# PEER selection over 64 candidate places in place of 256, and 16 dots moved one stage earlier

## The reference, cut to what matters

```
q = (xb @ w_q).reshape(t, 8, 2, 128)
s = einsum('thpd,hpkd->thpk', q, sub_keys)        # 8 heads x 2 sides x 128 scores per token
top_s, top_i = top_k(s, 16)                       # first selection, per side
cand_s = top_s[:, :, 0, :, None] + top_s[:, :, 1, None, :]   # 16 x 16 = 256 sums per head
best_s, best_pos = top_k(cand_s, 16)              # second selection
idx  = top_i[side 0] * 128 + top_i[side 1] at best_pos
gate = softmax(best_s)
h = gelu(u_table[idx] . xb)
out = sum_k gate * h * v_table[idx]
```

## Time and profile before

| what | us |
|---|---|
| median of 3 runs (lowest, highest) | 3355.05 (3344.94, 3362.86) |
| the profiled execution, its own time | 3345.05 |
| its span, first to last instruction | 3342.9 |
| PE busy | 2903.2 (87%) |
| DVE busy | 2117.9 (63%) |
| ACT busy | 1227.8 (37%) |
| POOL busy | 417.1 (12%) |

### The profile page before, as it was taken

One profiled execution on the slowest core, in us unless ns is written; L12 is line 12 of the kernel. 1 busy time (PEld: TensorE's weight loads), 2 busy tenths in 40 slices (PEclk: granted clock), 3 DMA queues, 4 the chain that ended last, 5 costly groups with the idle time before them and its releaser, 6 DMA issues. The chain is left out here.

```text
span 3342.9 us, 39660 instructions
## 1 busy us (share of the span) xinstructions
PE 2903.2 (87%) x14455; PEld 2351.1 (70%) x14455; DVE 2117.9 (63%) x3648; ACT 1227.8 (37%) x1680; POOL 417.1 (12%) x386
## 2 busy tenths in 40 slices
PE   7998889999939994788869699989998989998897
PEld 2875557777728652666658489989997977666676
DVE  2247348788832257544443426998888759888887
ACT  2248237777722333000032233333333333333232
POOL 0000010000010001000000000000100025555521
PEclk9999979999969856777779899999999989999999
DMA  7350459999913200000013134667776799999996
GB/s 255 95 202 28 132 227 373 369 370 375 353 63 94 71 0 6 1 0 0 0 47 98 57 112 133 203 200 232 236 229 183 216 314 396 390 387 380 380 355 242
DMA packets 370122, 652.22 MB, mean 195 GB/s; under 512 B 120864, under 2 KB 269600, under 8 KB 349088
## 3 DMA queue, kind: packets, MB, share of 16 engines
q1 hardware_dynamic: 225760, 458.09, 39.5%
q0 software_dynamic: 45792, 166.74, 13.5%
q10 hardware_dynamic: 98400, 25.17, 3.4%
HBM read 567.08 MB, written 82.84 MB: 194 GB/s over the span
## 5 line engine op out<-in xcount | busy, mean ns | idle before, releaser
L169 DVE TENSOR_TENSOR w_low<-raw,w_high 128x1024 fp32r<-128x1024 f32 x362 | 442.9, 1223 | 494.4 <-ACT w_high L160 491.8
L160 ACT CAST w_high<-raw 128x1024 fp32r<-128x1024 f32 x362 | 378.6, 1046 | 497.0 <-PE ps L329 481.5
L327 PE MATMUL ps<-x_high,w_high 128*128 128x384 f32 (+1 forms) x1328 | 466.8, 352 | 12.7 <-DVE x_low L2245 11.3
L329 PE MATMUL ps<-x_high,w_low 128*128 128x384 f32 (+1 forms) x1328 | 463.6, 349 | 0.0
L328 PE MATMUL ps<-x_low,w_high 128*128 128x384 f32 (+1 forms) x1328 | 463.4, 349 | 0.0
L266 DVE TENSOR_TENSOR wide_low<-wide_raw,wide_high 128x2048 fp32r<-128x2048 f32 x138 | 314.3, 2290 | 102.7 <-ACT wide_high L259 102.0
L2290 POOL DMA_INDIRECT sp_rows<-in_u_rows,sp_flat x128 | 187.0, 1461 | 1477.5 <-DVE sp_flat L2566 834.2
L327 PE MATMUL ps<-w_high,po_both_high 128*128 128x512 f32 x768 | 312.2, 407 | 50.9 <-DVE po_both_low L2751 50.8
L328 PE MATMUL ps<-w_low,po_both_high 128*128 128x512 f32 x768 | 306.4, 399 | 0.0
L329 PE MATMUL ps<-w_high,po_both_low 128*128 128x512 f32 x768 | 306.4, 399 | 0.0
L259 ACT CAST wide_high<-wide_raw 128x2048 fp32r<-128x2048 f32 x138 | 263.2, 1912 | 76.1 <-DMA wide_raw<-in_w_experts 57.0
(11 more groups left out here) (525 smaller groups left out, 5326.7 us busy)
## 6 DMA issues: line engine op xcount, KB each, us to landing
wide_raw<-in_w_experts SPq DMA_DIRECT2D x138, 1024.0 KB, 8.0
raw<-in_u SPq DMA_DIRECT2D x128, 512.0 KB
raw<-in_v SPq DMA_DIRECT2D x128, 512.0 KB
ada_raw<-in_ada_w SPq DMA_DIRECT2D x24, 1024.0 KB, 5.0
hbuf<-ph_h SPq DMA_DIRECT2D x128, 192.0 KB
gbuf<-ph_staged ACTq DMA_DIRECT2D x6, 4096.0 KB, 33.3
xT<-hbuf SPq DMA_DIRECT2D x128, 192.0 KB
xT<-gbuf SPq DMA_DIRECT2D x128, 192.0 KB
```

The source lines that it names most:

```text
L160: self.m.nc.scalar.copy(self.m.w_high[:, n % AHEAD, :], self.m.raw[:, n % RAW, :]).then_inc(self.m.high_done, 1)
L169: self.m.nc.vector.tensor_tensor(self.m.w_low[:, n % AHEAD, :], self.m.raw[:, n % RAW, :], self.m.w_high[:, n % AHEAD, :].bitcast(F32), AL ...
L327: nc.tensor.matmul(out, w[0], a[0], start=start, stop=False, **more)
L329: return nc.tensor.matmul(out, w[1], a[0], start=False, stop=stop, **more)
```

## The change

In `choose`, half 0 now makes the first selection for all 16 head sides (ten steps), and half 1 the second selection for all 8 heads. The second selection runs over the 64 places of four strips (first rank, number of ranks, width): 16 + 24 + 16 + 8 places, which hold every pair with (a+1)(b+1) at most 16. The place is turned back into the two ranks by two shifts and ten small float instructions. The comparison with 0 to 15 (`eq`) is made for all heads at once, one side after the other. `finish` and `place` stay. 64 dots are made in `peer_hidden` (four more in the choices c = 2 to 5, twelve in the `LAST_ROWS`) and 64 in `peer_output`, in seven rows of twelve, the last in row 108.

```
-CHOOSE_DOTS = {2: (4, 9), 3: (4, 9), 4: (1, 3, 5, 7, 9), 5: (1, 3, 5, 7, 9), 6: (1, 3, 5, 7, 9), 7: (1, 3, 5, 7, 9)}
-EARLY_DOTS = 48
+CHOOSE_DOTS = {2: (2, 5, 8), 3: (2, 5, 8), 4: (1, 3, 5, 7, 8, 9), 5: (1, 3, 5, 7, 8, 9), 6: (1, 3, 5, 7, 9),
+               7: (1, 3, 5, 7, 9)}
+EARLY_DOTS = 64
+PAIRS = 64
+STRIPS = ((0, 1, 16), (1, 3, 8), (4, 4, 4), (8, 8, 1))
...
+                if half == 0:
+                    for side in range(2):
...                      (max, match_replace, max, max_index, max_index for 8 head sides, step 5*side .. 5*side+4)
+                    return
+                nc.vector.tensor_copy(idxf[:], idx[:])
+                for a0, rows, width in STRIPS:
+                    ins = nc.vector.tensor_tensor(cand[...] of [P, HEADS, rows, width] ..., ALU.add)
+                link(ins)
+                every(HEADS, max over cand)            ; step(0)
+                every(HEADS, match_replace)            ; step(1)
+                every(HEADS, max over crest)           ; step(2)
+                every(HEADS, max_index over cand)      ; step(3)
+                every(HEADS, max_index over crest)
+                difference for the gates; two shifts; copies to float, two links
+                step(4)
+                ten small float instructions [P, 8, 16], seven links
+                step(5)
+                for side, out in enumerate((i_, j_)):
+                    link(is_equal into eq [P, 8, 16, 16])   ; step(6 + 2 * side)
+                    link(eq * indices)                      ; step(7 + 2 * side)
+                    link(tensor_reduce)
...
                 for _ in range(LAST_ROWS[c - CHOICES] if c >= CHOICES else 0):
                     row(r)
                     r += 1
+                    sparse.dot(dve, next(dots))
...
 def dot_rows():
-        if r % 6 != 5 and s < SLOTS_EACH:
+        if r * 7 // 12 != (r - 1) * 7 // 12 and s < SLOTS_EACH:
             rows[r].append(s)
```

More of the change, by code:

```diff
@@ L2332, in peer_hidden @@
     QUADS, QUADS_EACH = HALF_TILE // QUAD, ROUND // QUAD
-    K, HH = TOPK, HEADS // 2
+    K = TOPK
     BATCH = 16
@@ L2341, in peer_hidden @@
         rest = sb("rest", [P, HEADS, KEYS])
[L2342 to L2347, removed]
+        val, idx, idxf = (sb(n, [P, 2 * HEADS, K], dt) for n, dt in (("val", F32), ("idx", U32), ("idxf", F32)))
+        cand, crest = sb("cand", [P, HEADS, PAIRS]), sb("crest", [P, HEADS, PAIRS])
+        best, pos, part = sb("best", [P, HEADS, K]), sb("pos", [P, HEADS, K], U32), sb("part", [P, 2, HEADS, K], U32)
+        whole, parts, ranks = (sb(n, [P, a, HEADS, K]) for n, a in (("whole", 1), ("parts", 2), ("ranks", 2)))
+        e4 = crest[:].rearrange("p h c -> p (h c)").rearrange("p (a h k) -> p a h k", a=len(STRIPS), k=K)
+        eq = sb("eq", [P, HEADS, K, K])
         i_, j_, g_ = (sb(n, [P, 2, HEADS, K]) for n in "ijg")
@@ L2512, in choose @@
                 tt = ORDER[n]
-                mine = slice(half * HH, (half + 1) * HH)
-                gates_out = sparse.gate[:].rearrange("p (h k) -> p h k", k=K) if n == 0 else g_[:, (n - 1) % 2]
[L2515 to L2524, removed]
-                step(4)
-                link(nc.vector.tensor_copy(idxf[:], idx[:]))
-                pairs = val[:].rearrange("p (h s) k -> p h s k", s=2)
@@ L2528, in choose @@
[L2528 to L2531, removed]
-                step(5)
-                every(HH, lambda a: nc.vector.match_replace(crest[:, a, :], best[:, a, 0:8], cand[:, a, :], NEG))
@@ L2534, in choose @@
[L2534 to L2547, removed]
-                sides = idxf[:].rearrange("p (h s) k -> p s h k", s=2)
@@ L2549, in choose @@
[L2549 to L2555, removed]
@@ L2556, in choose @@
-                link(ins)
-                for side, out in enumerate((i_, j_)):
-                    ins = nc.vector.tensor_reduce(out[:, (n - 1) % 2, mine, :], eq[:, side], AX.X, ALU.add)
-                link(ins)
-                step(9)
+                if half == 0:
+                    for side in range(2):
+                        some = [side * HEADS + a for a in range(HEADS)]
+                        top = scores[:, tt]
+                        every(HEADS, lambda a: nc.vector.max(val[:, some[a], 0:8], top[:, some[a], :]))
+                        step(5 * side)
+                        every(HEADS, lambda a: nc.vector.match_replace(rest[:, a, :], val[:, some[a], 0:8],
+                                                                       top[:, some[a], :], NEG))
+                        step(5 * side + 1)
+                        every(HEADS, lambda a: nc.vector.max(val[:, some[a], 8:16], rest[:, a, :]))
+                        step(5 * side + 2)
+                        every(HEADS, lambda a: nc.vector.max_index(idx[:, some[a], 0:8], val[:, some[a], 0:8],
+                                                                   top[:, some[a], :]))
+                        step(5 * side + 3)
+                        every(HEADS, lambda a: nc.vector.max_index(idx[:, some[a], 8:16], val[:, some[a], 8:16],
+                                                                   rest[:, a, :]))
+                        step(5 * side + 4)
+                    return
@@ new lines, in choose @@
+                nc.vector.tensor_copy(idxf[:], idx[:])
+                pairs = val[:].rearrange("p (h s) k -> p h s k", s=2)
+                at = 0
+                for a0, rows, width in STRIPS:
+                    ins = nc.vector.tensor_tensor(
+                        cand[:, :, at:at + rows * width].rearrange("p h (a b) -> p h a b", b=width),
+                        pairs[:, :, 0, a0:a0 + rows].unsqueeze(3).to_broadcast([P, HEADS, rows, width]),
+                        pairs[:, :, 1, 0:width].unsqueeze(2).to_broadcast([P, HEADS, rows, width]), ALU.add)
+                    at += rows * width
@@ new lines, in choose @@
+                link(ins)
+                every(HEADS, lambda a: nc.vector.max(best[:, a, 0:8], cand[:, a, :]))
+                step(0)
+                every(HEADS, lambda a: nc.vector.match_replace(crest[:, a, :], best[:, a, 0:8], cand[:, a, :], NEG))
+                step(1)
+                every(HEADS, lambda a: nc.vector.max(best[:, a, 8:16], crest[:, a, :]))
+                step(2)
+                every(HEADS, lambda a: nc.vector.max_index(pos[:, a, 0:8], best[:, a, 0:8], cand[:, a, :]))
@@ new lines, in choose @@
+                step(3)
+                every(HEADS, lambda a: nc.vector.max_index(pos[:, a, 8:16], best[:, a, 8:16], crest[:, a, :]))
+                gates_out = sparse.gate[:].rearrange("p (h k) -> p h k", k=K) if n == 0 else g_[:, (n - 1) % 2]
+                nc.vector.tensor_tensor(gates_out, best[:], best[:, :, 0:1].to_broadcast([P, HEADS, K]), ALU.subtract
+                                        ).then_inc(diffed, 1)
+                for k, bits in enumerate((3, 2)):
+                    ins = nc.vector.tensor_scalar(part[:, k], pos[:], bits, None, ALU.logical_shift_right)
@@ new lines, in choose @@
+                nc.vector.tensor_copy(whole[:, 0], pos[:])
+                link(ins)
+                link(nc.vector.tensor_copy(parts[:], part[:]))
+                step(4)
+                p_, a_, b_ = whole[:, 0], ranks[:, 0], ranks[:, 1]
+                link(nc.vector.tensor_scalar(a_, parts[:, 0], -1.0, 0.0, ALU.add, ALU.max))
+                link(nc.vector.scalar_tensor_tensor(out=a_, in0=parts[:, 1], scalar=-6.0, in1=a_, op0=ALU.add, op1=ALU.max))
+                link(nc.vector.scalar_tensor_tensor(out=a_, in0=p_, scalar=-48.0, in1=a_, op0=ALU.add, op1=ALU.max))
@@ new lines, in choose @@
+                for k, (_, _, width) in enumerate(STRIPS):
+                    ins = nc.vector.scalar_tensor_tensor(out=e4[:, k], in0=a_, scalar=-float(width), in1=p_, op0=ALU.mult,
+                                                         op1=ALU.add)
+                link(ins)
+                link(nc.vector.scalar_tensor_tensor(out=b_, in0=e4[:, 1], scalar=-8.0, in1=e4[:, 0], op0=ALU.add,
+                                                    op1=ALU.max))
+                link(nc.vector.scalar_tensor_tensor(out=b_, in0=e4[:, 2], scalar=-24.0, in1=b_, op0=ALU.add, op1=ALU.max))
@@ new lines, in choose @@
+                link(nc.vector.scalar_tensor_tensor(out=b_, in0=e4[:, 3], scalar=-48.0, in1=b_, op0=ALU.add, op1=ALU.max))
+                step(5)
+                iota16 = m.iota[:, 0:K].unsqueeze(1).unsqueeze(1).to_broadcast([P, HEADS, K, K])
+                sides = idxf[:].rearrange("p (h s) k -> p s h k", s=2)
+                for side, out in enumerate((i_, j_)):
+                    link(nc.vector.tensor_tensor(eq[:], ranks[:, side].unsqueeze(3).to_broadcast([P, HEADS, K, K]), iota16,
+                                                 ALU.is_equal))
+                    step(6 + 2 * side)
+                    link(nc.vector.tensor_tensor(eq[:], eq[:], sides[:, side].unsqueeze(2).to_broadcast([P, HEADS, K, K]),
```

(3 more changed lines are left out.)

## The result

The changed kernel took 3315.2 us in the median of 4 runs (3308.4 to 3320.44), the kernel before 3349.99 (4 runs, 3342.16 to 3362.86): ratio 0.9889, 95% interval 0.9859 to 0.9919. In a second group of runs on one chip, 6 of the changed kernel against 11 of the one before, the ratio was 0.9925 (0.9906 to 0.9944). Both intervals hold the forecast, 3325 for 3355.05, which is 0.9910. The change is thus a gain of about 1%, clear of the noise.

The account below looks back on a forecast made before the run. Bounds: TensorE waiting for VectorE at the hidden stage's gates, DMA in the first 96 output rows. Choices -10, late rows +1, transition +5, output rows -26 make -30: median 3355.05 becomes 3325 us, range 3302 to 3349.

Parts of the forecast that it names:

- Choices, -10: Hidden stage: TensorE waits less for VectorE at the first gates of c = 4 to 7; -10 us, between -4 and -16.
- sum per tile: Selection on VectorE: cheaper maxima and sums, less ten added small instructions, net 7 us less per tile.
- Cost of an instruction over 64, 201 ns less than over 256: Selection on VectorE: a maximum over 64 saves 201 ns against one over 256; bounds 134 and 201.
- Late rows: Last hidden rows: twelve dots cost nothing by themselves, except 1.1 us at the gates of c = 9.
- Transition, +5: Hidden to output stage: six more gathers delay the last gate store in the open; 5 us, bounds 0 and 10.
- the turn-taking of the queues: Gate stores: each gather would delay a store by its whole transfer, 1.35 us; the total would be three us smaller.
- Output rows, -26: Output stage: fewer gather bytes at 386 GB/s, rows 4.53 us in place of 4.87; -26 us, bounds -63 and +9.
- The sum of -30: Whole kernel: -10 + 1 + 5 - 26, so its own execution goes from 3345 to 3315 us.
- The rival "latency": Output stage: landing time, not bytes, sets the row, which stays 4.86 us; 3360 us, slower than before; chance 0.10.

Follow-up runs that it names:

- g_balanced: Changed kernel with the odd choices' steps dealt out evenly and seven dots in late even choices, three in odd ones; 3304.3 us, ratio 0.9861.
- i_before_ring5: Kernel before with five slots in place of four for the rows of h and gates in the output stage; 3332.18 us, ratio 0.9945.
- a: Kernel before with the new selection alone, its dots left as they were; 3335.63 us, ratio 0.9964.
- f: Changed kernel with the six dots behind the gates of c = 9 moved into the choices; 3313.64 us, ratio 0.989.
- h: Changed kernel with even steps in odd choices, five slots for h and gates, and the six very last dots moved into the choices; 3286.61 us, ratio 0.9812.
- c: Changed kernel without the late gathers of u, dot instructions kept; one execution, output stage 543.3 us, rows 12 to 104 4.24 us each.
- d: Changed kernel with late dots cut to 16 of 1024 elements, all gathers kept; one execution, rows 12 to 104 4.41 us each.
- e: Changed kernel with five slots in place of four for the rows of h and gates in the output stage; 3306.17 us, ratio 0.9867.

## Why the prediction was right, and where its terms were off

- *Choices, -10: measured -11.* Losses forecast 4.8, 11.0, 4.1, 9.9; measured 4.4, 10.5, 3.6, 9.9. The step sums held because they added the cost step by step against TensorE's row, with the slack of light steps thrown away. A sum per tile (7 us less, so 28 for four) would have said more than twice too much. `g_balanced` shows that the odd choices' loss came from the order: the same work dealt out evenly gives another 13.7 us.
- *Cost of an instruction over 64, 201 ns less than over 256: measured 201.* The value at the one end of my bounds was right; there is no floor down to 64.
- *Late rows: the dots free, 1.1 at the gates of c = 9: measured 1.1.* From gelu to gelu the row there takes 12.66 us in place of 10.52, but the next one 3.16 in place of 4.16: that gelu stood 1.0 us behind four copies of ScalarE that waited for the first store, and TensorE did not wait for it. So TensorE's own loss went from 2.8 to 3.9 us, and the first store's delay was hidden, as forecast.
- *Transition, +5: measured +6.0, and the price of a gather was too low.* I had 0.9 us for each gather beside a store, from 35.3 against 32.4 and 32.8. The 32.8 was a high reading: the same store landed after 30.0 us in `i_before_ring5`, which differs from the kernel before in the output stage alone, after 30.4 in `a` and `f` and 30.1 in `h`, and with six more gathers after 38.8: 1.4 us each, the gather's own transfer at 386 GB/s (1.35). That the stretch came within 1 us of the forecast is in part luck: against the transition of `a` (10.4) or `i` (10.9) in place of 12.8, the six gathers cost 8 us. So the turn-taking of the queues in the Trainium skill's page "DMA: Bandwidth & Descriptors" (section "Queues, rings and completion order"), which I had weighed against the trace and set aside, fits the last store better. At the store of c = 8 the price was lower, 39.2 less 32.4 over six or 1.1 (a seventh was issued 2 us before the landing).
- *Output rows, -26: measured -18.9 in the first profile.* This term was over-sized by 7 us. Where it went: my 104 rows of 4.53 charged the first twelve rows with the steady price, and they took 57.8 us for 54.4, filling from empty as they did before; rows 12 to 104 took 4.56 for 4.53 (3.0); and the last 23, for which I wrote 4.2, took 98.3 for 96.6. The mechanism stood in its main part: taking the gathers away brings the row to 4.24 us, near TensorE's pace, and the same bytes at one more slot give the same 398 GB/s in both kernels. What the term had wrong is the fixed rate of 386: it depends on the lead, and taking the dots away raised it too (4.41). The rate also varies from run to run, 381 to 389 GB/s between executions that share the output stage's code, which is 4.48 to 4.59 us a row and 10 us of the stage (566.8 to 576.6).
- *The sum of -30* stands against 24.2 in the spans of the first profiles and 37 and 25 us in the two groups of timed runs. It lies between these two, which are themselves 12 us apart, so the runs bear out its size but not its last 5 us.
- *The rival "latency"* named a real thing and gave it a wrong form. The row did not stay at 4.86, so it was no replacement for the bytes; but the two-row lead costs some 3% of the rate in both kernels (386 and 382 to 389 GB/s against 398 and 399), and I had excluded that with the argument that 386 GB/s "is just what the bytes need". That is true of any rate, since a row's time times its rate always gives its bytes: the agreement showed nothing.

## What to carry to other kernels

Work placed between the rows of a pipeline is priced per step: what a step lacks to the row's length is lost, what it has over it piles up until the next wait, so the same sum of work is cheap when dealt out evenly and dear when heavy passes stand together at the end. A DMA rate read from a busy stretch is the rate of this depth of prefetch and no ceiling; before a stage is called bound by bytes, give its loads one more slot. Bytes moved ahead in front of a transfer that someone waits for can delay it by their full transfer time (1.1 to 1.4 us for each 0.52 MB here), so move them beside one that nobody waits for. And take the price of such a thing from more than one execution: the base of this forecast, 32.8 us, stood 2.4 to 2.8 us above what four other executions show.

## What the runs showed that I had not expected

- A DMA busy share of 1.01 at 386 GB/s was not full: 1.03 and 397 to 399 GB/s came with one more slot of lead, or (one execution) with a VectorE row some 0.6 us shorter on the average.
- The output stage of unchanged code varied by 10 us between executions with its DMA rate, while the hidden stage repeated within 0.8 us (661.2 to 662.0 us in the six profiles of the changed kernel, `c`, `d`, `e` and `f`, which share its order or nearly so). Differences under 10 us in the output stage can't be read from one profile.
- With the losses cut to some 4 us the granted clock of the windows at the first gates was 1.00 in three of four (`g`), where the changed kernel had 0.86, 0.81, 1.00 and 0.71; 1.00 is TensorE's level of 2.4 GHz, and a lower mean says that a part of the window ran at 1.2.
